# An encoder layer on eight cores: another set of seven products for the first FFN matmul, read from one accumulating bank, with staggered units

## What is computed

```
proj   = x @ w_in                      # conv input, q, k, v, memory q, gate logits
y_conv, y_attn, y_mem = convolution, windowed attention, memory attention
merged = sum_b sigmoid(gate_b) * y_b
x1     = LayerNorm(alpha * x + merged @ w_o)
gate, up = split(x1 @ w_ffn_in)        # 1024 -> 2 x 2816
out    = LayerNorm(alpha * x1 + (silu(gate) * up) @ w_ffn_out)
```

## Time and profile before

| what | us |
|---|---|
| median of 3 runs (lowest, highest) | 1074.12 (1072.76, 1075.02) |
| time of the profiled execution | 1074.63 |
| its span on the slowest core, 7 | 1073.5 |
| spans of the other cores | 1058.9 to 1072.4 |
| PE busy, share of the span | 983.4, 92% |
| DVE, ACT, POOL busy | 616.4, 408.4, 408.1 |

### The profile page before, as it was taken

The page is one execution under the profiler, slowest core; times in us unless marked ns, Lnnn a source line. Parts: engine busy times, 40 slices in busy tenths (PEclk is TensorE's granted clock), DMA queues, the critical chain, the costliest instruction groups (busy, mean ns, idle before and its releaser), DMA issues.

```text
span 1073.5 us, 16537 instructions; the slowest of 8 cores (1058.9 to 1073.5 us)
## 1 busy us (share of the span) xinstructions
PE 983.4 (92%) x5606; PEld 451.1 (42%) x5606; DVE 616.4 (57%) x971; ACT 408.4 (38%) x612; POOL 408.1 (38%) x363
## 2 busy tenths in 40 slices
PE   4899999998999999999987889888999899888996
PEld 1355545443444444444443334333444344333442
DVE  1324576565743433534599865777755546886464
ACT  1135675655632222222254444333221444333221
POOL 3200000211343343433255557676632565554331
PEclk9999999998999999999999899999999999999999
DMA  8996033824389669532765456755333533120222
GB/s 125 167 171 129 7 104 83 134 54 78 62 124 155 160 129 174 139 87 89 223 232 197 133 186 162 152 125 146 119 127 110 195 137 129 59 79 1 79 99 79
DMA packets 42610, 132.57 MB, mean 123 GB/s; under 512 B 5280, under 2 KB 17192, under 8 KB 41600
## 3 DMA queue, kind: packets, MB, share of 16 engines
q1 hardware_dynamic: 29936, 90.35, 25.4%
q0 software_dynamic: 12592, 41.16, 24.5%
HBM read 141.93 MB, written 35.18 MB: 165 GB/s over the span
## 4 chain that ended last, share of the span: by engine, by line
PE 66%; DVE 12%; DMA 8%; issue 6%; POOL 4%; ACT 3%; SPq 0%; DVEq 0%; POOLq 0%; ACTq 0%
PE ps L234 65%; DVE arena L1062 4%; DVE arena L1222 3%; DMA arena<-w_out 2%; DVE arena L819 2%; POOL arena L1212 1%; POOL arena L1208 1%; DMA arena<-w_q 1%; DMA arena<-xt 1%; DMA arena<-u_scratch 1%; DVE arena L1066 1%; ACT arena L1201 1%; DVE arena L817 1%; DMA gexp_scratch<-arena 1%; DMA arena<-x 1%
## 5 line engine op out<-in xcount | busy, mean ns | idle before, releaser
L234 PE MATMUL ps<-arena 128*128 128x512 bf16 (+5 forms) x5196 | 966.8, 366 | 77.9 <-DVE arena L819 24.2
L234 PEld LDWEIGHTS ps<-arena 128*128 128x128 bf16 (+2 forms) x5196 | 431.0, 99 | 596.6 <-issue 156.5
L1222 DVE TENSOR_TENSOR arena<-arena,ps 128x512 f32<-128x512 f32 x176 | 114.5, 681 | 93.0 <-POOL arena L1212 90.7
L866 DVE SCALAR_TENSOR_TENSOR arena<-arena,ps 128x512 f32<-128x512 f32 x96 | 65.3, 684 | 112.8 <-PE ps L234 106.9
L845 ACT ACTIVATE arena<-ps,bgate_sb 128x512 f32<-128x512 f32 x96 | 65.6, 687 | 169.4 <-PE ps L234 158.5
L1201 ACT COPY arena<-ps 128x512 f32<-128x512 f32 x132 | 77.1, 587 | 77.5 <-PE ps L234 68.9
L1208 POOL TENSOR_TENSOR arena<-arena 128x512 f32<-128x512 f32 x44 | 61.1, 1389 | 114.8 <-ACT arena L1201 114.8
L1044 ACT ACTIVATE arena<-arena 128x1024 bf16<-128x1024 f32 x32 | 33.8, 1056 | 118.8 <-DVE arena L1290 98.5
L873 POOL TENSOR_TENSOR arena<-arena 128x512 f32<-128x512 f32 x32 | 40.8, 1274 | 97.8 <-DVE arena L866 97.7
L148 POOL DMA_DIRECT2D arena<-w_g x21 | 11.3, 544 | 170.3 <-PE ps L234 169.2
L1071 POOL TENSOR_TENSOR arena<-arena 128x1024 f32<-128x1024 f32 (+1 forms) x24 | 59.9, 2499 | 41.8 <-ACT arena L1070 41.8
(11 more groups left out here) (106 smaller groups left out, 610.6 us busy)
## 6 DMA issues: line engine op xcount, KB each, us to landing
arena<-w_forms SPq DMA_DIRECT2D x24, 896.0 KB, 5.5
w_forms<-arena SPq DMA_DIRECT2D x12, 896.0 KB, 4.0
arena<-w_bf_cache SPq DMA_DIRECT2D x20, 512.0 KB, 3.6
arena<-u_scratch SPq DMA_DIRECT2D x64, 135.0 KB, 3.1
arena<-x SPq DMA_DIRECT2D x16, 512.0 KB, 9.8
y_scratch<-arena SPq DMA_DIRECT2D x16, 512.0 KB, 5.3
arena<-y_scratch SPq DMA_DIRECT2D x16, 512.0 KB, 3.7
out<-arena SPq DMA_DIRECT2D x16, 512.0 KB, 2.6
```

Source lines behind the costliest of these rows:

```text
L234: return pe.run(lambda: nc.tensor.matmul(out, lhsT, rhs, start=start, stop=stop, skip_group_check=onto), deps, inc)
L866: t_y = dve.run(lambda: nc.vector.scalar_tensor_tensor(out=gb[r], in0=gb[r], scalar=1.0, in1=ps[:, bk, :], op0=ALU.add, op1=ALU.mult), [tk ...
L1222: return dve.run(lambda: nc.vector.tensor_tensor(out=dst, in0=dst, in1=ps[:, b, :], op=op), deps)
```

## The change

- `f1_unit` becomes `f1_period(cur, prev)`. A period makes three products of the unit `cur` and the last four of the unit before, `prev`; units thus overlap by a period. A unit's seven products are another set (Winograd's form), in the order M1 (form 0, A11), form 3 with A12, form 6 with SA1 in its first period, and form 5, form 4, form 1 and form 2 in its second, each in turns with those of its neighbour.
- Bank x of a unit accumulates four products, and ACT reads it between them: after the first (`t1`), after form 6 (`tu`) and after form 5 (`t3`). The banks y and z hold what DVE adds to those copies (`plus`). POOL has no more additions, only three products of gate and up per pair; DVE has one.
- `fold` has three dependent steps. It is called for every unit of both passes, for `cur + 2`, at the end of a period. `FG`, `fold_load`, `fold_sum`, `fold_step` and `w1_forms` go; all 22 weight units go through `w1_bf16_cache`. There are four weight buffers; units 0 and 1 of pass 0 are loaded and summed during `c_main` 3.
- `e_sums` has four steps of 128 x 2048 in sequence; one overwrites A21 in place.
- x has 16 buffers; four of them are loaded during `c_main` 3, twelve after it.
- In stage D the scaling is never done on DVE, and `d_tiny(k + 1)` comes right before `d_Y(k + 1)` where `d_tiny(k + 2)` stood behind it. In F1 the chain steps come in every odd unit from 1 to 11.
- The last unit of a pass (`f1_drain`) has 15 matmuls of the first F2 block between its products.

```diff
-    NFOLD = 12
-    w1c = {"j": NFOLD}
+    w1c = {"j": 0}
     def fold(buf, dep):
-        t1 = ... out=G[:, 4:6, :], in0=G[:, 2:4, :], in1=twice(0), op=ALU.add), [dep])
-        dve.run(... out=G[:, 6, :], in0=G[:, 1, :], in1=G[:, 0, :], op=ALU.subtract))
-        return dve.run(... out=G[:, 2:4, :], in0=G[:, 2:4, :], in1=twice(1), op=ALU.add), [t1])
+        t1 = ... out=G[:, 4:6, :], in0=G[:, 1:3, :], in1=G[:, 0:2, :], op=ALU.subtract), [dep])
+        t2 = ... out=G[:, 6, :], in0=G[:, 2, :], in1=G[:, 4, :], op=ALU.subtract), [t1])
+        return ... out=G[:, 1, :], in0=G[:, 3, :], in1=G[:, 6, :], op=ALU.subtract), [t2])
...
-            if v < NFOLD:
-                w1_tok[u] = dma(sp, w1s[r], w1f_d[v], w1_slot[r], [w1_free[r], fold_st[v]])
-            else:
-                w1_tok[u] = dma(sp, w1s[r][:, 0:4], w1b_d[v], w1_slot[r], [w1_free[r], w1_raw[v]])
+            w1_tok[u] = dma(sp, w1s[u % 4][:, 0:4], w1b_d[u % 22], w1_slot[u % 4], [w1_free[u % 4], w1_raw[u % 22]])
     def fold_w1(u):
-        if u < 44 and u % 22 >= NFOLD:
-            w1_tok[u] = fold(w1s[u % 3], w1_tok[u])
+        if u < 44:
+            w1_tok[u] = fold(w1s[u % 4], w1_tok[u])
...
+    def f1_period(cur, prev, fill=lambda: None):
+        if cur is not None:
+            load_w1(cur + 2)
...
+            t = prod(s["x"], W, 0, A11, True, [dx, w1_tok[cur], t_x1T[8 * P:8 * P + 8]])
+            s["t1"] = grab(s["T"][0], s["x"], [t, free.get("11"), tg0])
+        if prev is not None:
...
+            t = prod(q["x"], Wq, 5, S3q, False, [q["tu"], sa[3]])
+            q["t3"] = grab(q["T"][2], q["x"], [t, c_free[upq]])
+        fill()
+        if cur is not None:
+            y, dy = banks.alloc(1)
+            t = prod(y, W, 3, A12, True, [dy])
+            s["c11"] = plus(s["T"][0], y, [t, s["t1"]])
...
+        if prev is not None:
+            z, dz = banks.alloc(1)
+            t = prod(z, Wq, 4, SA[:, 0], True, [dz, sa[1]])
+            q["c22"] = plus(q["T"][2], z, [t, q["t3"]])
+            fill()
+        if cur is not None:
+            t = prod(s["x"], W, 6, SA[:, 1], False, [s["t1"], sa_tok[P][2]])
+            s["tu"] = grab(s["T"][1], s["x"], [t, free.get("12"), tg0])
...
+        if prev is not None:
+            t = prod(q["x"], Wq, 1, A22q, False, [q["t3"]])
...
+            t = prod(z, Wq, 2, SA[:, 2], False, [q["c22"], sa[4]])
+            w1_free[prev % 4] = [t]
+            q["c12"] = plus(q["T"][1], z, [t, q["tu"]])
...
+        if cur is not None:
+            fold_w1(cur + 2)
```

More of the change, by code:

```diff
@@ L993, in _build @@
     load_wos(2, [])
-    fold_load(1)
-    straight(cat([c_main(1, tt) for tt in range(4)]), True)
+    cache_w1(4)
+    straight(cat([c_main(1, tt) for tt in range(4)]))
     load_wg(3, [pe.tok()])
@@ L998, in _build @@
     t_wo = load(w_o_sb, w_o_d, [a_done])
-    straight(cat([c_main(2, tt) for tt in range(4)]), True)
+    cache_w1(3)
+    straight(cat([c_main(2, tt) for tt in range(4)]))
     dp2_done = pe.tok()
@@ new lines, in e_sums, with f1_operands, prod @@
+        t4 = sub(SA[:, 2], A12, SA[:, 1], [t2])
+        sa_tok[P] = [None, t1, t2, t3, t4]
+    t_free = {}
+    unit = {}
+    silu12 = []
+    def f1_operands(u):
+        P, v = u // 22, u % 22
+        return (P, v // 2, v % 2, w1s[u % 4], x1T[:, P, 0, 0:4, :], x1T[:, P, 0, 4:8, :],
+                x1T[:, P, 1, 0:4, :], x1T[:, P, 1, 4:8, :])
+    def prod(b, W, form, rhs, first, deps):
+        for kc in range(4):
+            tk = mm(ps[:, b, :], W[:, form, kc, :], rhs[:, kc, :], first and kc == 0, kc == 3,
+                    deps if kc == 0 else (), inc=(kc == 3), onto=not first)
+        return tk
@@ new lines, in grab, with plus, silu, times @@
+    def grab(buf, b, deps):
+        return act.run(lambda: nc.scalar.copy(buf, ps[:, b, :]), deps)
+    def plus(buf, b, deps):
+        return dve.run(lambda: nc.vector.tensor_tensor(out=buf, in0=buf, in1=ps[:, b, :], op=ALU.add), deps)
+    def silu(buf, src, deps):
+        return act.run(lambda: nc.scalar.activation(buf, src, AF.Silu), deps)
+    def times(dst, up, gate, deps, eng=None):
+        if eng is None:
+            return pool.run(lambda: nc.gpsimd.tensor_tensor(out=dst, in0=up, in1=gate, op=ALU.mult), deps)
+        return dve.run(lambda: nc.vector.tensor_tensor(out=dst, in0=up, in1=gate, op=ALU.mult), deps)
@@ L1330, in _build @@
             e_start()
-            e_sums(0, [c_done])
+            e_sums(0, [c_done] + [x1_free[i] for i in range(4)])
         d_H(tb)
@@ L1334, in _build @@
             d_chain(False)
-    w2_order = list(range(8, 22)) + list(range(8))
+    tg0 = [z_free, c_done, g_done, [x1_free[tb] for tb in range(4)]]
+    w2_order = list(range(22))
     for u in range(22):
-        f1_unit(u)
-        if u % 3 != 2 and chain["k"] < 18:
+        f1_period(u, u - 1 if u else None)
+        if u % 2 and chain["k"] < 18:
             d_chain(True)
-        if u >= 8:
+        if u >= 11:
             for _ in range(2):
```

291 lines of the change are left out of this document (120 added, 171 removed).

## The result

The changed kernel takes 1047.67 us (median of four runs), the kernel before, run beside it, 1074.49 us. The ratio is 0.9745, with a 95% interval of 0.9725 to 0.9765: 27 us faster, where 25 were forecast. Its profiled execution took 1045.4 us with a span of 1044.4 us on core 0, the slowest; before it was 1073.5 us, so the two spans differ by 29.1 us.

A forecast was written before the change was run, and what follows sets the result against it. PE, busy 92% of the span, was taken as the bound. Terms of -6.3, -4.1, +10.7, -16.0 and -9.4 sum to -25.1 us, from 1074.63 to 1049.5, median 1049; own range 1042 to 1058, 8 in 10 within 1035 to 1067.

The forecast's parts named there:

- The bound: Whole kernel: PE, busy for 92% of the span, sets the time; gain only from its idle or slow-clocked time.
- `c_main` and the start of D: Up to the fourth residual sum of stage D: early weight sums and stores go, x is resident; gain 6.3 us.
- The rest of D: Fourth residual sum to the token sums: rounds of 4.3 us, one without a chain of 3.5; gain 4.1 us.
- First two units of pass 0: Start of F1: DVE's queue and unit 2's late weight load idle PE some 7 us, then a 1.7 us dip.
- S: Start of the token sums, at the end of stage D; 585.71 us in the kernel before.
- Periods 2 to 11: Pass 0 with the chain: PE waits 1.8 and 0.6 us per pair; five pairs of 15.2 us, 1 for the clock.
- Units 12 to 21: Pass 0 after the chain: sums end in time, 0.2 us lost per pair; 66.8 us for 82.8, gain 16.0.
- rival of the slower side: F1, both passes: the fold stays the limit in every unit, now made in all 44; 1099 us, chance 7%.
- Pass 1: Second pass of F1: a late weight load costs 10.5 us and a dip; 147.4 us against 156.8, gain 9.4.
- (1): Rival: PE never waits for DVE outside the two starts, so stage D and chain pairs are faster; 1035 us, chance 17%.
- (2): Rival: loads are later still; 2 us and a dip in five chain pairs give 17 us more, 1066 us, chance 15%.
- (4): Rival: the change only moves waits, as starts and chain pairs lose more; time within 0.2% of before, chance 3%.

The follow-up runs named there:

- old tiny order: The changed kernel with the tiny instructions of stage D behind the centring again, all scalings on ACT and POOL: 1040.4 us, ratio 0.9682.

## Why the prediction was right, point by point

**The bound.** Right. PE was the pace, and its idle and slow-clocked time the only thing to win; its work is the same and the span is 29.1 us shorter.

**`c_main` and the start of D.** Right in size, -5.9 for -6.3, and the first sum is at 514.06 where near 514 was forecast. For the 7.57 us wait the reason was wrong: it went with the weight sums and stores in SP's queue, not with resident tiles. Of the 5.9 us, 2.3 are the last gate product coming at 510.61 and not 512.95, as the wait of `c_main` had it (medians of the eight cores 506.4 and 508.2). The row that could have told me is in the queue of SP, and I had read only the one of DVE, "ended by DMA x".

**The rest of D.** Wrong: +2.0 for -4.1. The step that failed is "ACT comes to the scale about 2.3 us into the round, so POOL's 2.36 us fall after the centring". The scale waits for the last centring alone and so starts 0.17 us into the round (566.48, the residual sum at 566.31). POOL's add then starts 1.5 us in, where the tiny instructions stand. I had let only large instructions of DVE lose time to POOL. Nine of the eleven rounds with a chain cost 5.18 us instead of 4.3. The round without a chain took 1.14 us and not 3.5 (residual sums at 550.51 and 551.65), which hid 2.4 us of that.

**First two units of pass 0.** Right in size: from S to the transposes of period 1 are 602.22 + 0.85 - 581.86 = 21.2 us, forecast 19.0 + 1.7. But the one gap of 7 us was two, 8.78 us before the third product and 3.43 us behind the load; the early load removed the second and left the first. I had POOL's add and the sums in DVE's queue and not in PE's wait: S is when the first sum starts, and PE goes on 6.0 us later (587.85), when ACT has copied what that add let it copy. The dip behind it cost 2.7 us and not 1.7.

**Periods 2 to 11.** The mechanism was right, both waits of a pair and their releasers; the term was mis-sized: 69.3 us for 77.0. Pairs with centring take 14.6, 14.9 and 14.7 us (forecast 15.2), but there are three of them and not five. The last centring, of block 15, runs in period 6; behind it DVE has one scaling, in period 8, and periods 8 to 11 go at 12.5 us per pair. That was to be had by counting. The 1 us for the clock wasn't paid either.

**Units 12 to 21.** Right: -18.1 for -16.0, without the 18.9 us that were lost before. The fold with one POOL product ends in time, and that run puts its cover at 0.4 us, where 0.0 was forecast and 0.2 per pair taken as the loss. The rival of the slower side (folds stay the limit, 1099 us) is refuted with pairs at 12.1 us; but the run with the long step made three times shows how near it stands: 1.6 us more per pair, and the time is above the kernel before.

**Pass 1.** Right: -10.7 for -9.4. The load behind the store of F2's last block made a gap of 6.96 us (7 to 8 forecast), and an early load removed it, for 9.1 us. It was issued 11.4 us after the start of the pass (11.6 forecast) and landed 4.5 us later. Unforeseen are the 2.51 and 1.19 us in front of it, ended by ACT's copies, which stand behind the last block's LayerNorm.

**The other rivals.** PE does wait for DVE in the chain pairs, so (1) is out, though the total lies 1 us on its side of the forecast. The loads land at 4.1 us in the median (3.6 before), so (2) is out too; its own sum was short, since 2 us and a dip of 1.7 in five pairs are 18.5 us and not 17. (4) is out by the time itself.

That 1049 met 1047.7 so closely owes something to luck: stage D was 6.1 us worse than forecast and the stretch from S to 320 matmuls 7.2 us better. Without either error the forecast would have been 1047.9; with only one of them it would have been 6 or 7 us away, inside 1035 to 1067 still, but in one case just below the 1042 of my own range.

**Open.** Which part of the change freed the sums from PE's path, as said above. Of the 3 us that the old tiny order takes off behind S, 1.3 are that PE goes on 4.7 us after S and not 6.0 (587.04 and 582.38 there), and the rest was not followed. Whether the token sums can come before the last residual sums, which would take out the largest gap left, wasn't tried.

## What to carry to other kernels

When sums move into a pipeline, don't count them: find the product that reads one and ask what stands between the end of the sum and that product, in the same queue. A load or store issued in order behind something that waits has a latency that no DMA row shows; read the queue of the issuer around each stage's seam, and move the issue ahead of the waiting one. And when two engines share a lock, a tiny instruction can lose as much as a large one, in every round, because the delay itself sets the phase of the next meeting. And where a wait is for two things, look for both in the code before you believe the name in the row.

## What the runs showed of the hardware

**The lock between DVE and POOL doesn't look at size.** The timeline of the changed kernel in pass 1, a step of a fold with POOL idle and a fold with POOL's product beside it; these rows answer to the earlier trace rows.

```profile
884.83 0.42 DVE L807 TENSOR_TENSOR arena<-arena 128x512 bf16<-128x512 bf16 x1
...
890.38 1.53 POOL L1169 TENSOR_TENSOR arena<-arena 128x512 bf16<-128x512 f32 x1 [1.24 <-DVE arena L1162]
890.88 1.31 DVE L807 TENSOR_TENSOR arena<-arena 128x512 bf16<-128x512 bf16 x1
892.29 0.42 DVE L808 TENSOR_TENSOR arena<-arena 128x512 bf16<-128x512 bf16 x1
```

One of three steps loses a turn, 1.31 for 0.42 us, until POOL's product is over; it is never more than one, as POOL has one operation there: of the 44 folds of this core 17 have one long step and 27 none. The prediction took 1.3 us for it and the row shows 0.9. POOL's product itself takes 1.53 instead of 1.28 us where it starts while L806 still runs (until 890.77). In stage D L1028 took 2.13 us for 0.16 in the same way. This bears out the Trainium skill, "SBUF — State Buffer", section on the two separate sides: the loser waits for the whole instruction of the other. That the loser may be an instruction on 128x1 numbers follows from it, but it took this trace to make me count it.

**Short waits that return did not bring the clock down here.** The windows of the stretch after the 8.78 us gap and of two chain pairs in the changed kernel, with the columns of the earlier trace rows, and behind them of pass 1 with the long step made three times.

```profile
587.85:603.00 15.15, 11.55 (x39) 4.65 (x41) 7.65 (x14) 6.20 (x10) 1.82 (x2) 0.73 0.30 104
617.64:632.58 14.94, 12.79 (x66) 5.78 (x65) 10.30 (x19) 7.28 (x13) 4.37 (x4) 1.00 0.31 106
632.58:647.29 14.71, 12.75 (x65) 5.78 (x65) 10.30 (x19) 6.71 (x11) 4.37 (x4) 1.00 0.31 108
```

```profile
889.77:932.77 43.00, 38.89 (x176) 16.61 (x175) 34.76 (x56) 18.04 (x32) 12.17 (x9) 1.00 0.24 74
```

With 1.43 and 0.66 us of waiting in every pair, and with 1.09 and 0.21, the granted clock stays at 1.00, which is 2.4 GHz. After the gap of 8.78 us the mean is 0.73: part of the stretch runs at 1.2 GHz, and 27 matmuls take 9.28 us from 587.85, against 6.20 for 28. The Trainium skill, "TensorE: Matmul & The Clock Gate", section on oscillation, describes waits for DMAs, longer than these, that bring the clock down in each round. These waits didn't; those of 3.01 us in the earlier trace rows did.
